# Expert gates of a PEER layer: two added 128-column products per token in place of one of 256 columns

## The chip, the cores and the metric

The kernel runs on one core of a Trainium2 chip. The core has TensorE (PE; its weight loads are the row PEld), VectorE (DVE), ScalarE (ACT), GpSimd (POOL), and SyncE (SP), which issues most transfers. The metric is the device time of one execution in microseconds. Before the change it was 1377.74 us in the median of 3 runs (1374.68 to 1379.49).

## The reference, cut to what matters

The program computes two transformer blocks for 256 tokens of width 1024. The last part of the second block is the PEER layer, a layer of 128 x 128 = 16384 experts:

```
s = einsum('thpd,hpkd->thpk', q, sub_keys)            # 8 heads, 2 halves, 128 keys
top_s, top_i = top_k(s, 16)
cand_s = top_s[:, :, 0, :, None] + top_s[:, :, 1, None, :]
cand_i = top_i[:, :, 0, :, None] * 128 + top_i[:, :, 1, None, :]
best_s, best_pos = top_k(cand_s, 16)                  # 8 x 16 = 128 picks per token
gate = softmax(best_s)
h = gelu(einsum('thkd,td->thk', u_table[idx], xb))
return einsum('thk,thkd->td', gate * h, v_table[idx])
```

Each pick is an expert (i, j) with a gate. All values are 32-bit floats.

## The kernel before, in words

For 224 of the 256 tokens (`TD`) the PEER layer is computed densely. `u_table` and `v_table` are read whole, as 128 items of 128 x 1024 each, one item for each value of j (for v: likewise). For each u item TensorE computes the pre-activations of 128 experts for 224 tokens; ScalarE applies gelu and writes them to the tile `HS`, which is 128 values of i on the partitions by 128 values of j by 224 tokens. Then `HS` must be multiplied by the gates, which are zero for all but the 128 picks of a token. The remaining 32 tokens are computed with gathered rows by GpSimd's indirect transfers and VectorE.

All products take 32-bit operands as a high part and a low part, since the fast product format keeps only some of the bits. An item of weights lands in `RAW` (a ring of 4 slots, transfers issued by SP at line 411), ScalarE makes its high part `WH` (line 1043 in this stage), GpSimd the low part `WL` (line 455), and TensorE does three products for each of the 8 chunks of 128 rows (line 1179): high x high, high x low, low x high, each with 224 columns. That is 24 products for an item.

The gates of a token are made as a product of one-hots (`gates_of`, line 1742). The contraction is over the token's 128 picks: `hot_i` has a 1 where the pick's i is, `hot_j` has the gate where the pick's j is. `hot_j` holds the gate's high part (VectorE, line 2546) and its low part (ScalarE, line 1019). One product per token has `hot_i` as the stationary operand and both parts of `hot_j`, side by side, as 256 moving columns, so that PSUM gets two halves of 128 columns that have still to be added.

The tokens are worked in groups of four, which I call a step: index c in the code, in two halves g of two tokens a. There are 224 / 4 = 56 steps. The order is written out by hand. In the last part of the u items (the one-hot stage) each item on TensorE has the four tokens of one step in its middle: 12 products of the item, 4 of one-hots, 12 of the item. TensorE's loop waits for `hot_low` (the low parts are there) and `gated` (VectorE is done with the step two before, whose PSUM banks are used again). ScalarE does in an item: the copy of the parked half of a step (`rest_high`, line 1010), the low parts (line 1019), the high part of an item (line 1043), and after each second item a gelu (line 995). VectorE does in a step the one-hots of the next (`one_hots`, lines 2543 and 2546), then `gate`: only 64 of the 128 values of j (`KEPT`) are multiplied at once, because `HS` holds items whose gelu is done; the other 64 are parked in a tile `stage` and in DRAM, and multiplied in the next stage.

In `gate` before the change VectorE sums the halves of the 64 kept j (line 2558, a reduction of 512 elements to 256 into PSUM bank 2), adds the low half of the 64 parked j to the copy of the high half that ScalarE has put into `stage` (line 2561), and multiplies `HS` by the sums (line 2563).

After this stage comes the v stage: 128 items, for each 8 pairs of products, one of 448 columns (line 1802) and one of 224 (line 1803).

Of the kernel before, what the change touches and what calls it, by code (L numbers as in the profile page):

```python
# [19 lines left out]
ALU = mybir.AluOpType  # L20
# [5 lines left out]
AX_X = mybir.AxisListType.X  # L26
# [24 lines left out]
PH, NK, TOPK = 8, 128, 16  # L51
# [9 lines left out]
KEPT = 64  # L61
# [88 lines left out]
def bass_blocks(nc, weights, x_in, p_in, vec_in, rows_in, gate_w_in, lora_in, mb_in, fb_in, out, rest_dram, x2_dram, u_rows):  # L150
    with ExitStack() as ctx:
# [158 lines left out]
        hot_i = at("hot_i", [P, 2, 2, P], F32R, C0 + 1024)  # L310

        hot_j = at("hot_j", [P, 2, 2, 2, NK], F32R, 0)
        stage = at("stage", [P, 2, NK - KEPT, 8], F32, 4096)
# [14 lines left out]
        PS = ctx.enter_context(nc.psum_tensor("PS", [P, 8, 512], F32))  # L328
# [6 lines left out]
        def sem(name):  # L335
            name = LATER[name][0] if name in LATER else name
            if name not in sems:
                sems[name] = ctx.enter_context(nc.semaphore(name))
            return sems[name]
# [44 lines left out]
            i = n - FIRST["keys"]  # L384
            return KK[:, 1, i, :] if 0 <= i < 2 else WL[:, n % RING, :]

        def made(c, part_):
            b = 4 + 2 * (c % 2)
            return PS[:, b:b + 2, :].rearrange("p b (a l j) -> p l j (b a)", a=2, l=2)[:, part_]

        def at_token(x, t):
            return x[:, t:t + 1] if isinstance(t, int) else x[:, bass.ds(t, 1)]
# [149 lines left out]
        def _(act):  # L542
# [107 lines left out]
            for e in range(2 * MH):  # L650
# [5 lines left out]
                for sb in range(NT):  # L656
                    last = A(WE[:, e % 2, sb, :], PS[:, 6 + h % 2, d * S:(d + 1) * S], ACT.Relu,
                             bias=AT[:, 2 * d + sb, h:h + 1])
# [346 lines left out]
            def rest_high(i, c, first=False):  # L1005

                act.wait_ge(sem("hot_used"), 8 * i + (2 * c + 2))
                if c % 2 == 0 and not first:
                    act.wait_ge(sem(f"parked{c // 2}"), 16 * i)
                nc.scalar.copy(stage[:, c // 2, :, 4 * (c % 2):4 * (c % 2) + 4],  # L1010
                               made(c, 0)[:, KEPT:NK]).then_inc(sem("rest_high"), 1)

            def hot_lows(i, c):

# [132 lines left out]
        def _(pe):  # L1147
# [584 lines left out]
            def gates_of(i, c, first=False):  # L1732

                if not first:

                    pe.wait_ge(sem("gated"), 4 * i + (c - 1))
                elif c >= 2:
                    pe.wait_ge(sem("gated"), c - 1)
                for g in range(2):
                    pe.wait_ge(sem("hot_low"), 8 * i + (2 * c + g + 1))  # L1740
                    for a in range(2):
                        last = mm(PS[:, 4 + 2 * (c % 2) + g, a * 2 * NK:(a + 1) * 2 * NK], hot_i[:, g, a, :],  # L1742
                                  hot_j[:, g, a, :, :], start=True, stop=True)
                    last.then_inc(sem("hot_used"), 1)

            def gates_behind(i, c):
# [114 lines left out]
        def _(dve):  # L1861
# [688 lines left out]
            def gate(i, c, first=False):  # L2550

                dve.wait_ge(sem("hot_used"), 8 * i + (2 * c + 2))
                hs = HS[:, 0:KEPT, tokens(16 * i + 4 * c, 4)]
                kept, parked = slice(0, KEPT), slice(KEPT, NK)
                dve.wait_ge(sem("rest_high"), 4 * i + (c + 1))
                b = 4 + 2 * (c % 2)
                sums = PS[:, 2, 2 * NK * (c % 2):2 * NK * (c % 2) + 4 * KEPT].rearrange("p (j a) -> p j a", a=4)
                V.tensor_reduce(sums, PS[:, b:b + 2, :].rearrange(
                    "p b (a l j) -> p j (b a) l", a=2, l=2)[:, kept], AX_X, ALU.add).then_inc(sem("sums_ready"), 1)
                rest = stage[:, c // 2, :, 4 * (c % 2):4 * (c % 2) + 4]  # L2560
                V.tensor_tensor(rest, rest, made(c, 1)[:, parked], ALU.add)
                dve.wait_ge(sem("sums_ready"), 4 * i + (c + 1))
                V.tensor_tensor(hs, hs, sums, ALU.mult).then_inc(sem("gated"), 1)

            def rest_block(r):

# [170 lines left out]
```

## Time and profile before

| | |
|---|---|
| median of 3 runs | 1377.74 us |
| the profiled execution's own time | 1376.38 us |
| its span in the trace | 1374.6 us |
| PE busy, of the span | 1337.0 us, 97% |
| DVE busy | 952.6 us, 69% |
| ACT busy | 848.9 us, 62% |
| POOL busy | 842.2 us, 61% |
| one-hot stage | 846.6 to 1027.4 us of the span |
| v stage | about 1029 to 1362 us |

The span is the stretch from the first to the last instruction in the trace; 1.8 us of the execution lie outside it. Matmuls are pipelined: the trace gives each a duration of 220 to 450 ns, but they start 60 to 240 ns apart, so that a mean duration is not what a product costs. What it costs is the distance from its start, or from the start of its weight load, to the next one's. An engine's busy time is the time in which at least one of its instructions is under way.

### The profile page before, as it was taken

The page shows a single profiled execution, that of the slowest core. Times are in us where ns is not written, and L with a number is a line of the kernel's source. Part 1 is how long each engine was busy: PE and PEld are TensorE (multiplying, and loading weights), DVE is VectorE, ACT ScalarE, POOL GpSimd, SP SyncE. Part 2 cuts the span into 40 slices and gives each one's busy share as a digit, 9 for nine tenths or more (in the row PEclk, how much of TensorE's full clock was granted, in tenths as well). Part 3 has the DMA queues.
Part 4 walks back from the last instruction along what each step waited for, and adds up shares of the span by engine and source line. Part 5 has one row for each costly group of instructions (what it writes and reads, how often), then busy time and mean ns, then how long its engine had stood idle before and what let it go on. Part 6 is the DMA issues. An engine that isn't in the chain of part 4 may idle for free.

```text
span 1374.6 us, 28810 instructions
## 1 busy us (share of the span) xinstructions
PE 1337.0 (97%) x9930; PEld 1215.8 (88%) x9930; DVE 952.6 (69%) x1998; ACT 848.9 (62%) x1463; POOL 842.2 (61%) x410
## 2 busy tenths in 40 slices
PE   7999999999999999989999989999999999999996
PEld 6878888888898777879999989999999999999996
DVE  3784884024674664453999465999997988888885
ACT  5475775445865656555777736888885554555553
POOL 7885888887675622867999848777772222233310
PEclk9999999999999999999999999999999999999998
DMA  6643555654443421655566577565657999898981
GB/s 205 206 135 126 172 197 196 196 189 156 167 158 116 143 78 46 214 185 167 186 200 196 187 291 257 200 201 198 204 199 286 345 365 369 310 331 315 328 290 61
DMA packets 83838, 287.68 MB, mean 209 GB/s; under 512 B 9656, under 2 KB 10040, under 8 KB 83512
## 3 DMA queue, kind: packets, MB, share of 16 engines
q1 hardware_dynamic: 64192, 231.76, 50.1%
q0 software_dynamic: 9216, 33.56, 6.3%
q10 hardware_dynamic: 10360, 21.43, 4.5%
q8 instruction: 43, 0.70, 0.2%
q14 instruction: 27, 0.22, 0.1%
HBM read 277.23 MB, written 9.44 MB: 209 GB/s over the span
## 4 chain that ended last, share of the span: by engine, by line
PE 64%; POOL 12%; issue 8%; DVE 7%; DMA 6%; ACT 1%; ACTq 0%; POOLq 0%; DVEq 0%; SPq 0%
PE PS L1179 37%; POOL WL L455 12%; PE PS L1802 10%; PE PS L1803 5%; DMA RAW<-weights 3%; PE PS L1742 2%; PE PS L1224 2%; DMA stage_odd<-gates_rest 2%; DVE WL L2636 2%; PE PS L1225 1%; PE PS L1561 1%; DVE gathered L2587 1%; DMA gathered<-u_rows,chosen 1%; PE PS L1519 0%; DVE XS L2417 0%
## 5 line engine op out<-in xcount | busy, mean ns | idle before, releaser
L455 POOL TENSOR_TENSOR WL<-RAW,WH 128x1024 fp32r<-128x1024 f32 x294 | 709.0, 2424 | 243.2 <-ACT WH L550 181.0
L1179 PE MATMUL PS<-XHL,WH 128*128 128x224 f32 (+1 forms) x2528 | 438.1, 278 | 8.6 <-DVE WL L2611 6.4
L1179 PEld LDWEIGHTS PS<-XHL,WH 128*128 128x128 f32 x2528 | 388.3, 193 | 12.4 <-DVE WL L2611 6.8
L1179 PE MATMUL PS<-XHL,WL 128*128 128x224 f32 (+1 forms) x1264 | 350.2, 277 | 0.0
L1802 PE MATMUL PS<-CHL,WH 128*128 128x448 f32 x1024 | 322.0, 375 | 1.4 <-DVE CHL L2575 1.4
L1803 PE MATMUL PS<-CHL,WL 128*128 128x224 f32 x1024 | 270.6, 264 | 0.0
L550 ACT CAST WH<-RAW 128x1024 fp32r<-128x1024 f32 x184 | 191.2, 1047 | 106.2 <-PE PS L1179 96.4
L1179 PEld LDWEIGHTS PS<-XHL,WL 128*128 128x128 f32 x1264 | 244.1, 193 | 0.0
L1084 ACT CAST WH<-RAW 128x1024 fp32r<-128x1024 f32 x128 | 134.8, 1053 | 150.3 <-PE PS L1803 80.3
L1802 PEld LDWEIGHTS PS<-CHL,WH 128*128 128x128 f32 x1024 | 192.1, 188 | 16.7 <-DVE CHL L2575 1.6
L1803 PEld LDWEIGHTS PS<-CHL,WL 128*128 128x128 f32 x1024 | 195.4, 191 | 0.0
L2636 DVE TENSOR_TENSOR WL<-RAW,WH 128x1024 fp32r<-128x1024 f32 x128 | 156.5, 1223 | 43.5 <-ACT WH L1084 42.7
L1043 ACT CAST WH<-RAW 128x1024 fp32r<-128x1024 f32 x124 | 129.0, 1043 | 64.3 <-PE PS L1179 51.7
L1224 PE MATMUL PS<-XHL,WH 128*128 128x512 f32 x384 | 138.4, 403 | 0.5 <-DVE XHL L2431 0.4
L511 POOL DMA_INDIRECT gathered<-weights,chosen x32 | 54.0, 1688 | 110.3 <-DVE sparse_y L2602 78.0
L1179 PE MATMUL PS<-WH,XHL 128*128 128x512 f32 x352 | 118.9, 402 | 0.6 <-POOL WL L455 0.4
L511 POOL DMA_INDIRECT gathered<-u_rows,chosen x32 | 51.1, 1597 | 109.5 <-DVE gathered L2587 100.7
L1225 PE MATMUL PS<-XHL,WL 128*128 128x256 f32 x384 | 108.1, 282 | 0.0
L1019 ACT ACTIVATE hot_j<-hot_j,GQ 128x128 fp32r<-128x128 f32 x224 | 78.0, 395 | 26.9 <-DVE hot_j L2546 25.4
L1224 PEld LDWEIGHTS PS<-XHL,WH 128*128 128x128 f32 x384 | 72.8, 190 | 18.3 <-issue 1.2
L1179 PEld LDWEIGHTS PS<-WH,XHL 128*128 128x128 f32 x352 | 66.5, 189 | 16.8 <-POOL WL L455 1.1
L2546 DVE TENSOR_SCALAR hot_j<-PS,JT,GH 128x128 fp32r<-128x128 f32 x224 | 80.6, 401 | 0.0
(433 smaller groups left out, 2120.5 us busy)
## 6 DMA issues: line engine op xcount, KB each, us to landing
RAW<-weights SPq DMA_DIRECT2D x438, 512.0 KB, 3.8
gates_rest<-stage ACTq DMA_DIRECT2D x28, 256.0 KB, 2.2
stage<-gates_rest ACTq DMA_DIRECT2D x7, 512.0 KB, 9.1
stage_odd<-gates_rest ACTq DMA_DIRECT2D x7, 512.0 KB, 8.2
H<-x SPq DMA_DIRECT2D x2, 512.0 KB, 4.5
LG<-rows ACTq DMA_DIRECT2D x2, 512.0 KB, 6.4
LB<-rows ACTq DMA_DIRECT2D x2, 512.0 KB, 9.2
x<-H ACTq DMA_DIRECT2D x1, 1024.0 KB, 5.7
```

The lines of the kernel that those rows point to most:

```text
L455: nc.gpsimd.tensor_tensor(WL[:, slot, :], RAW[:, slot, :], plain(WH[:, slot, :]), ALU.subtract).then_inc(w_lo, 1)
L511: nc.gpsimd.indirect_dma_start(out=gathered[:, n % ROWS, :], out_offset=None, in_=table, in_offset=bass.IndirectOffsetOnAxis(ap=chosen[:, ...
L550: nc.scalar.copy(high_of(n), RAW[:, slot, :]).then_inc(w_hi, 1)
L1043: nc.scalar.copy(WH[:, slot, :], RAW[:, slot, :]).then_inc(w_hi, 1)
L1084: nc.scalar.copy(WH[:, slot, :], RAW[:, slot, :]).then_inc(w_hi, 1)
L1179: last = mm(dst, a, b, start=start and k == 0, stop=stop and k == len(pairs) - 1)
L1224: mm(both, wh, XHL[:, :, k, :], start=(k == 0), stop=False)
L1225: last = mm(PS[:, bank, 0:S], wl, XH[:, k, :], start=False, stop=(k == KC - 1))
L1802: mm(PS[:, ch, 0:2 * TD], wh, CHL[c][:, :, :].rearrange("p a t -> p (a t)"), start=start, stop=False)
L1803: return mm(PS[:, ch, 0:TD], wl, CHL[c][:, 0, :], start=False, stop=stop)
L2546: last = V.tensor_scalar(hot_j[:, g, a, 0, :], iota_ps, at_token(JT, t + a), at_token(plain(GH), t + a), ALU.is_equal, ALU.mult)
L2636: V.tensor_tensor(WL[:, slot, :], RAW[:, slot, :], plain(WH[:, slot, :]), ALU.subtract).then_inc(w_lo, 1)
```

## The change

Each token gets two products of 128 columns in place of one of 256: both with the same stationary operand `hot_i`, the first with the high part of `hot_j`, the second with the low part, and the second adds to the same 128 columns of PSUM. The four tokens of a step then take one PSUM bank and not two, and what is in PSUM is the finished gate. So VectorE's reduction and its addition into `stage` go, and the multiplication reads PSUM's gates directly. ScalarE's copy into `stage` stays, of the same size, and now copies the finished gates. The helper `made` loses its argument for the half. The waits between the engines stay; only the one of VectorE for its own reduction (`sums_ready`) goes.

```diff
--- before.py
+++ after.py
@@ -384,9 +384,8 @@
             i = n - FIRST["keys"]
             return KK[:, 1, i, :] if 0 <= i < 2 else WL[:, n % RING, :]
 
-        def made(c, part_):
-            b = 4 + 2 * (c % 2)
-            return PS[:, b:b + 2, :].rearrange("p b (a l j) -> p l j (b a)", a=2, l=2)[:, part_]
+        def made(c):
+            return PS[:, 4 + c % 2, :].rearrange("p (a j) -> p j a", a=4)
 
         def at_token(x, t):
             return x[:, t:t + 1] if isinstance(t, int) else x[:, bass.ds(t, 1)]
@@ -1008,7 +1007,7 @@
                 if c % 2 == 0 and not first:
                     act.wait_ge(sem(f"parked{c // 2}"), 16 * i)
                 nc.scalar.copy(stage[:, c // 2, :, 4 * (c % 2):4 * (c % 2) + 4],
-                               made(c, 0)[:, KEPT:NK]).then_inc(sem("rest_high"), 1)
+                               made(c)[:, KEPT:NK]).then_inc(sem("rest_high"), 1)
 
             def hot_lows(i, c):
 
@@ -1739,8 +1738,9 @@
                 for g in range(2):
                     pe.wait_ge(sem("hot_low"), 8 * i + (2 * c + g + 1))
                     for a in range(2):
-                        last = mm(PS[:, 4 + 2 * (c % 2) + g, a * 2 * NK:(a + 1) * 2 * NK], hot_i[:, g, a, :],
-                                  hot_j[:, g, a, :, :], start=True, stop=True)
+                        made_at = PS[:, 4 + c % 2, (2 * g + a) * NK:(2 * g + a + 1) * NK]
+                        mm(made_at, hot_i[:, g, a, :], hot_j[:, g, a, 0, :], start=True, stop=False)
+                        last = mm(made_at, hot_i[:, g, a, :], hot_j[:, g, a, 1, :], start=False, stop=True)
                     last.then_inc(sem("hot_used"), 1)
 
             def gates_behind(i, c):
@@ -2551,16 +2551,8 @@
 
                 dve.wait_ge(sem("hot_used"), 8 * i + (2 * c + 2))
                 hs = HS[:, 0:KEPT, tokens(16 * i + 4 * c, 4)]
-                kept, parked = slice(0, KEPT), slice(KEPT, NK)
                 dve.wait_ge(sem("rest_high"), 4 * i + (c + 1))
-                b = 4 + 2 * (c % 2)
-                sums = PS[:, 2, 2 * NK * (c % 2):2 * NK * (c % 2) + 4 * KEPT].rearrange("p (j a) -> p j a", a=4)
-                V.tensor_reduce(sums, PS[:, b:b + 2, :].rearrange(
-                    "p b (a l j) -> p j (b a) l", a=2, l=2)[:, kept], AX_X, ALU.add).then_inc(sem("sums_ready"), 1)
-                rest = stage[:, c // 2, :, 4 * (c % 2):4 * (c % 2) + 4]
-                V.tensor_tensor(rest, rest, made(c, 1)[:, parked], ALU.add)
-                dve.wait_ge(sem("sums_ready"), 4 * i + (c + 1))
-                V.tensor_tensor(hs, hs, sums, ALU.mult).then_inc(sem("gated"), 1)
+                V.tensor_tensor(hs, hs, made(c)[:, 0:KEPT], ALU.mult).then_inc(sem("gated"), 1)
 
             def rest_block(r):
```

On TensorE, in the loop over the one-hot stage, this is the middle of one item and its step of one-hots. `XHL` is the activations' high and low part, `WH` and `WL` the item's; a row without a count is one instruction. Before:

```order
L1179 MATMUL PS<-XHL,WH 128x224 x2
L1179 MATMUL PS<-XHL,WL 128x224
L1736 ISA
L1740 ISA
L1742 MATMUL PS<-hot_j,hot_i 128x256 x2
L1740 REGISTER_ALU
L1742 MATMUL PS<-hot_j,hot_i 128x256 x2
L1179 MATMUL PS<-XHL,WH 128x224 x2
L1179 MATMUL PS<-XHL,WL 128x224
```

In the changed program the same place reads (line numbers are one less, as the file is shorter):

```order
L1178 MATMUL PS<-XHL,WL 128x224
L1735 ISA
L1739 ISA
L1742 MATMUL PS<-hot_j,hot_i 128x128
L1743 MATMUL PS<-hot_j,hot_i 128x128
L1742 MATMUL PS<-hot_j,hot_i 128x128
L1743 MATMUL PS<-hot_j,hot_i 128x128
L1739 REGISTER_ALU
L1742 MATMUL PS<-hot_j,hot_i 128x128
L1743 MATMUL PS<-hot_j,hot_i 128x128
L1742 MATMUL PS<-hot_j,hot_i 128x128
L1743 MATMUL PS<-hot_j,hot_i 128x128
```

Four products have become eight; the waits (ISA, REGISTER_ALU) stand where they stood.

On VectorE, in the loop over the same stage, this is the end of one set of one-hots and `gate` of the step before. Before:

```order
L2546 TENSOR_SCALAR hot_j<-PS,JT,GH 128x128
L2555 ISA
L2558 TENSOR_REDUCE PS<-PS 128x256
L2561 TENSOR_TENSOR stage<-stage,PS 128x64x4
L2563 REGISTER_ALU
L2563 TENSOR_TENSOR HS<-HS,PS 128x64x4
L2540 REGISTER_ALU
```

In the changed program:

```order
L2546 TENSOR_SCALAR hot_j<-PS,JT,GH 128x128
L2554 ISA
L2555 REGISTER_ALU
L2555 TENSOR_TENSOR HS<-HS,PS 128x64x4
L2540 REGISTER_ALU
```

The reduction and the addition are gone, and the multiplication comes right behind the one-hots.

## Rows read from the trace of the kernel before

**Rows 1.** Page, part 1: busy time, share, instructions.

```profile
PE 1337.0 (97%) x9930; PEld 1215.8 (88%) x9930; DVE 952.6 (69%) x1998; ACT 848.9 (62%) x1463; POOL 842.2 (61%) x410
```

**Rows 2.** Stretches: window, length, busy time per engine, granted clock, DMA share, GB/s.

```profile
846.60:1027.38 180.78, 180.60 (x1548) 176.88 (x1548) 178.28 (x495) 155.31 (x360) 131.87 (x55) 1.00 0.59 198
...
1120.00:1160.00 40.00, 40.00 (x257) 38.18 (x257) 32.77 (x47) 19.28 (x29) 9.46 (x7) 1.00 0.99 375
```

**Rows 3.** Waits, 846 to 1030 us: total us, times, longest.

```profile
PEld PS L1742 <- ACT hot_j L1019: 2.8, 13, 0.3
...
DVE hot_i L2543 <- PE PS L1742: 1.1, 3, 0.7
```

**Rows 4.** Groups of instructions, 846 to 1030 us: busy us, mean ns | idle before.

```profile
L1179 PE MATMUL PS<-XHL,WH 128*128 128x224 f32 x902 | 153.7, 274 | 0.0
L1179 PEld LDWEIGHTS PS<-XHL,WH 128*128 128x128 f32 x902 | 137.2, 192 | 0.0
...
L1742 PE MATMUL PS<-hot_j,hot_i 128*128 128x256 f32 x224 | 42.5, 300 | 0.2
L2558 DVE TENSOR_REDUCE PS<-PS 128x256 f32<-128x512 f32 x56 | 38.5, 687 | 1.3 <-ACT stage L1010 1.3
L1742 PEld LDWEIGHTS PS<-hot_j,hot_i 128*128 128x128 f32 x224 | 33.0, 190 | 3.9 <-ACT hot_j L1019 2.8
L2561 DVE TENSOR_TENSOR stage<-stage,PS 128x256 f32<-128x256 f32 x56 | 22.9, 408 | 0.0
```

**Rows 5.** Chain that ended last, 867 to 883 us: start, us, what.

```profile
869.59 0.53 PE PS L1742 x4
870.12 2.67 PE PS L1179 x24
872.79 0.24 PE PS L1742 x2
873.03 0.03 issue
873.06 0.51 PE PS L1742 x2
...
876.24 0.53 PE PS L1742 x4
...
879.44 0.62 PE PS L1742 x4
```

**Rows 6.** Weight loads in order of time, end of the v stage: start, us.

```profile
1355.79 0.14 PEld L1835 LDWEIGHTS PS<-unit,dense_y 128*128 128x128 f32 x1
1355.90 0.30 PEld L1836 LDWEIGHTS PS<-unit,dense_y 128*128 128x128 f32 x2
1356.12 0.19 PEld L1802 LDWEIGHTS PS<-CHL,WH 128*128 128x128 f32 x1
1356.23 0.19 PEld L1803 LDWEIGHTS PS<-CHL,WL 128*128 128x128 f32 x1
```

**Rows 7.** The same view at 606 us, products of 256 and 128 columns alternating.

```profile
606.04 0.19 PEld L1718 LDWEIGHTS PS<-KK,QH 128*128 128x128 f32 x1
606.16 0.19 PEld L1719 LDWEIGHTS PS<-KK,QL 128*128 128x128 f32 x1
...
606.51 0.19 PEld L1224 LDWEIGHTS PS<-XHL,WH 128*128 128x128 f32 x1
```

**Rows 8.** The same view in the v stage, pairs of 448 and 224 columns.

```profile
1100.07 0.19 PEld L1802 LDWEIGHTS PS<-CHL,WH 128*128 128x128 f32 x1
...
1102.89 0.19 PEld L1802 LDWEIGHTS PS<-CHL,WH 128*128 128x128 f32 x1
```

**Rows 9.** VectorE in order of time, 878 to 880 us.

```profile
878.59 0.69 DVE L2558 TENSOR_REDUCE PS<-PS 128x256 f32<-128x512 f32 x1
879.19 0.41 DVE L2561 TENSOR_TENSOR stage<-stage,PS 128x256 f32<-128x256 f32 x1
879.52 0.41 DVE L2563 TENSOR_TENSOR HS<-HS,PS 128x256 f32 x1
879.85 0.41 DVE L2543 TENSOR_TENSOR hot_i<-PS,IT 128x256 fp32r<-128x256 f32 x1
```

## The prediction

> **What bounds the kernel now.** I first read the page's busy times: PE is busy 97% of the span, DVE 69% [rows 1]. A share over the whole span doesn't say what bounds the stage of the change, so I next read that stage alone, as a window. From the first one-hot product at 846.6 us to the end of the last at 1027.38 us PE is busy 180.60 of 180.78 us, and DVE 178.28 [rows 2]. The reader is to see two things in that row: PE has no idle time left, and DVE nearly none, so either could set the pace. DMA is at 0.59 of its share there, so no transfer does.
>
> The view of waits tells the two apart only in part. PE's weight loads wait 2.8 us in total for the low parts of `hot_j`, in 13 places, one in four of the 56 steps; DVE waits 1.1 us for PE [rows 3]. The chain of waits shows the pattern. It runs on PE: 24 products of an item take 2.67 us, then come the four of one-hots, and four successive steps of these take 0.53, 0.24 + 0.03 + 0.51 = 0.78, 0.53 and 0.62 us [rows 5]. That is 2.46 us for four steps. With 4 x 2.67 = 10.68 it makes 13.14 us for four steps, and 14 times that is 184 us, which agrees with the window's 180.78 (its first item is cut off). So PE sets the pace, and in one step of four it waits a quarter of a microsecond for one-hots that DVE and ACT bring late.
>
> DVE's own pace, from start to start: the reduction 879.19 - 878.59 = 0.60 us, the addition 0.33, the multiplication 0.33 [rows 9]. That the step's other work fills the rest follows from DVE being busy 178.28 us, 3.2 us for each of 56 steps; PE's is 180.78 / 56 = 3.2 too. The two are matched to within some hundredths of a microsecond, which is why PE's waits are so small.
>
> **What a product costs.** All rests on this. A matmul's mean duration (300 ns for one-hots [rows 4]) isn't its cost, as the next starts long before it ends. I take distances from start to start.
> - An item's products, 224 columns: 2.67 / 24 = 111 ns [rows 5].
> - 448 and 224 columns in turn: nine pairs from 1100.07 to 1102.89 us, 313 ns a pair, so some 202 ns for 448 columns if the 224 take 111 [rows 8]. Beyond 224 columns the cost grows by (202 - 111) / 224 = 0.41 ns a column.
> - 128 columns: at the end of the v stage one transposition and two ordinary products of 128 columns stand in a row. Their three weight loads and that of the next product start from 1355.79 to 1356.12 us, 0.33 / 3 = 110 ns each [rows 6]. In the stage of scores, 256 and 128 columns in turn, four loads take 606.51 - 606.04 = 0.47 us, 117 ns each [rows 7].
>
> So between 128 and 256 columns the cost is nearly flat, 110 to 120 ns: 128 columns are not cheaper than 224. What is common to these products is the weight load of 128 columns; there is one for every product, even where two in a row have the same stationary operand, as an item's first two have (902 loads for 902 products with `WH` [rows 4]; the two are high x high and high x low).
>
> I take 110 ns for a new product, the value of the row that is nearest in shape (128 columns, same stationary size, on a busy PE at full granted clock). The bounds are 71 ns below (the column price of [rows 8] carried on down from 224: 111 - 96 x 0.41) and 130 ns above (the one-hots' own 0.53 / 4 in an undisturbed step [rows 5], wait included).
>
> The Trainium skill's page "TensorE: Matmul & The Clock Gate", section "LDWEIGHTS (loading the stationary operand)", gives the load as columns by 1.2 GHz, an estimate of 107 ns for 128 columns; by it eight products cost 0.86 us. The same page's section "Back-to-back issue gap" speaks against that: it has 81 ns for each load and product of 128 columns in a sustained stream, and by it the eight would cost 0.65 us; the row of three 128-column products, at 110 ns, agrees with the first and not with the second. What hangs on the second is the rival of cheap products below.
>
> **The change part by part.**
> 1. TensorE: 224 products of 256 columns become 448 of 128. In a step, the undisturbed 0.53 us for four is 4 x 117 ns (the price in [rows 7]) and 0.06 us of issue and semaphores between the halves. Eight at 110 ns with the same 0.06 make 0.94 us. The step with 0.62 us has some 0.09 us more, put down to nothing that waits; I keep that once in four steps. Four steps: 4 x 0.94 + 0.09 = 3.85 us, against 2.46. That is 1.39 us more for four steps, if the wait of [rows 3] goes, and x 14 = 19.5 us.
> 2. VectorE: the reduction and the addition go, 0.60 + 0.33 = 0.93 us of a step [rows 9]; in busy time that is part of 38.5 + 22.9 us [rows 4]. DVE then needs 3.2 - 0.93 = 2.27 us for a step, against 2.67 + 0.94 = 3.61 us on PE. It is no longer near the bound, so the saving itself is worth nothing but the wait that goes: 0.78 - 0.53 = 0.25 us in one step of four, 3.5 us in 14, which the sum of point 1 has already taken in. Worth of this edit at the least 0, at the most 3.5 us.
> 3. Could the one-hots be late in another way? `hot_i` and `hot_j` have a buffer per half. PE now frees the first half 0.47 us after it begins a step and the second after 0.94. DVE's two halves of one-hots take (3.2 - 0.60 - 0.33 - 0.33) / 2 = 0.97 us each, so they are made by 0.47 + 1.94 = 2.4 us, and ACT's two low parts of the second half are there some 1 us later, 3.4. PE asks for them at 3.61 + 0.47 = 4.1. That leaves 0.7 us, room for ACT's gelu (0.53 us) ahead of them. It's enough, so I forecast no wait; if the quarter microsecond stays after all, 3.5 us are to be added.
> 4. The multiplication reads PSUM with the tokens 128 elements apart, and not in a row. The addition that goes read PSUM in just that way, and takes as long, 0.33 us to the next [rows 9]. Cost 0; if it doubled, DVE still had a microsecond of room.
> 5. ScalarE's copy has the same size; cost 0. The PSUM write of the second product adds onto the first's columns right behind it; an item's 24 products all do that at 111 ns, so 0.
> 6. After the stage: the v stage is PE's too (40.00 of 40.00 us [rows 2]), and starts after the last u item, so a longer stage moves it as a whole. DMA is at 0.99 of its share there, but the ring of four items can't carry transfers ahead from a stage that has DMA to spare. Nothing is given back, at most 1 to 2 us of odd waits.
>
> Sum against the profiled execution's own 1376.38 us: + 19.5 - 1 (half of the odd waits) = 1394.9 us. The median of the runs is 1.4 us above that execution, so in the runs' terms it is 1396.2. I say 1395.5.
>
> **The rivals.**
> - *Cheap products.* The weight load hides behind the product before, and cost follows columns down to 71 ns. Then a step's eight take 0.57 + 0.06, four steps 4 x 0.63 + 0.09 = 2.61 us, + 0.15 x 14 = 2 us: 1378.5 us, no measurable change. For it: the column price of [rows 8] holds above 224. Against it: [rows 6]. By the skill's 81 ns it would be an estimate of + 6.6 us, from the page "TensorE: Matmul & The Clock Gate". Chance 4%, and 3% for a value between the two prices, up to + 12 us.
> - *Faster.* The second product of a token has the stationary operand that is loaded already. If that load cost nothing, a token's pair would cost what its 256 columns cost now, four steps 4 x 0.53 + 0.09 = 2.21 us against 2.46, since DVE's relief takes PE's wait away: - 3.5 us, 1372.9 us. It decides from where the second product costs less than about 15 ns beyond the first. Against it: 902 loads for 902 products, and 111 ns each in the items, where two in three have the same case. Chance 3%.
> - *Dearer products.* The new ones cost as much as the present 256-column ones in place, 130 ns, with the waits kept: four steps 4 x 8 x 0.13 + 0.09 + 0.25 = 4.50 us, + 2.04 x 14 = 28.6 us, 1405 us. For it: the one-hots are the only products here that are spaced 130 ns. Against it: that spacing has the issue gap in it. Chance 8%.
> - *Relief that counts.* The change does what its words say and DVE, not PE, sets the pace. Then 56 x 0.93 = 52 us would go. PE's 180.60 of 180.78 us rule it out; it gets nothing beyond the 3% above.
>
> **How the numbers follow.** The forecast (+ 15 to + 23 us) has 82%: 1391 to 1400. The range for 8 in 10 takes a part of the dearer case and a little below: 1388 to 1401. A difference under 0.3%, 4 us, can't be told from no change. Slower by more than that: 82 + 8 + most of the 3 between = 92%. Within it: 5%. Faster: 3%.
>
> **What would show it.** In the changed profile: 448 one-hot loads and products; in the chain pieces of 0.9 to 1.0 us for eight products between pieces of 2.67 us; the one-hot stage near 199 us with PE still busy throughout, DVE at some 130 us (2.27 x 56); the wait for `hot_j` gone; the v stage as long as before. Wrong would be: weight loads of one-hots 55 to 80 ns apart (cheap products), fewer loads than products (faster), a new wait of PE on ACT, or a v stage that is shorter by what the stage before lost.

## The result, and the profile after

The changed kernel takes 1393.8 us in the median of 4 runs (1391.31 to 1394.9), against 1378.47 us for the kernel before (4 runs). The ratio is 1.0121, with a 95% interval of 1.01 to 1.0142: it is slower by 15.3 us. The forecast was 1395.5 us, 1.7 above the measured median, and inside its range of 1388 to 1401. The sum behind it, + 18.5 us, was 3.2 us too large.

The profiled execution took 1391.31 us, with a span of 1389.6 us. This is the busy line of its page.

```profile
PE 1351.9 (97%) x10154; PEld 1235.2 (89%) x10154; DVE 904.9 (65%) x1886; ACT 851.7 (61%) x1463; POOL 843.1 (61%) x410
```

Against [rows 1], TensorE has 224 instructions more and 14.9 us more busy time, VectorE 112 instructions and 47.7 us less. A twentieth of VectorE's work is gone, and the kernel is slower by about the time that was added to TensorE's.

The stage itself, as a window from the first one-hot product to the last (window, length, busy time of PE, weight loads, DVE, ACT and POOL, granted clock, DMA share, GB/s), answers to [rows 2]:

```profile
846.10:1043.90 197.80, 197.80 (x1772) 197.66 (x1771) 129.63 (x385) 158.98 (x361) 133.41 (x57) 1.00 0.55 184
```

It is 17 us longer. DVE has fallen from 178.28 to 129.63 us, and PE has no gap at all; even its weight loads now fill the window (197.66 of 197.80, against 176.88 of 180.78). The waits of the stage (total us, times, longest), which answer to [rows 3], have turned round. VectorE now waits for TensorE in all but one of its steps, and the wait of TensorE for `hot_j` is no longer in the view:

```profile
DVE hot_i L2543 <- PE PS L1743: 66.8, 55, 1.4
```

The groups of the stage (busy us, mean ns | idle before) that answer to [rows 4]:

```profile
L1743 PE MATMUL PS<-hot_j,hot_i 128*128 128x128 f32 x224 | 53.2, 276 | 0.0
...
L1743 PEld LDWEIGHTS PS<-hot_j,hot_i 128*128 128x128 f32 x224 | 43.0, 192 | 0.0
L1742 PEld LDWEIGHTS PS<-hot_j,hot_i 128*128 128x128 f32 x224 | 43.0, 192 | 0.1
```

448 products and 448 loads: the second product of a token loads the same stationary operand again. What each costs is best seen in the weight loads in order of time (start, us), a whole step of one-hots between two parts of an item:

```profile
878.25 0.19 PEld L1178 LDWEIGHTS PS<-XHL,WL 128*128 128x128 f32 x1
878.37 0.19 PEld L1742 LDWEIGHTS PS<-hot_j,hot_i 128*128 128x128 f32 x1
878.48 0.19 PEld L1743 LDWEIGHTS PS<-hot_j,hot_i 128*128 128x128 f32 x1
...
879.15 0.19 PEld L1743 LDWEIGHTS PS<-hot_j,hot_i 128*128 128x128 f32 x1
879.26 0.30 PEld L1178 LDWEIGHTS PS<-XHL,WH 128*128 128x128 f32 x2
```

From 878.37 to 879.26 are eight loads in 0.89 us, 0.11 us each. There is no gap between the two halves, where a wait stands in the program: the wait costs nothing when what it waits for is there. The chain of waits agrees with it; its pieces of 24 products (start, us) now come at a steady distance:

```profile
872.34 2.72 PE PS L1178 x24
...
875.91 2.72 PE PS L1178 x24
...
879.49 2.72 PE PS L1178 x24
```

3.57 us a step, that is 32 products at 111.7 ns. Before, four steps took 13.14 us, 3.28 each [rows 5].

What TensorE waited for before is plainer in the weight loads than in the view of waits, which lists only the longer gaps. Two steps of the kernel before: the low parts of the second half on ScalarE, and the first load of that half on TensorE (start, us).

```profile
882.00 0.69 ACT L1019 ACTIVATE hot_j<-hot_j,GQ 128x128 fp32r<-128x128 f32 x2 [0.27 <-DVE hot_j L2546]
882.75 0.30 PEld L1742 LDWEIGHTS PS<-hot_j,hot_i 128*128 128x128 f32 x2
```

```profile
885.43 0.70 ACT L1019 ACTIVATE hot_j<-hot_j,GQ 128x128 fp32r<-128x128 f32 x2 [0.28 <-DVE hot_j L2546]
886.18 0.30 PEld L1742 LDWEIGHTS PS<-hot_j,hot_i 128*128 128x128 f32 x2 [0.22 <-ACT hot_j L1019]
```

ScalarE is done at 882.69 and at 886.13, and TensorE goes on 0.05 us later both times. It is so in 54 of the 56 steps of the kernel before, not in one of four. The second load of a first half and the first of the second are there 0.17, 0.27, 0.17 and 0.42 us apart in turn, against 0.12 where nothing is late (e7 below): 0.5 us of waiting in four steps. In the changed kernel it is so in one step of 56, and the low parts lie ready 0.34 us early.

**The balance.** I take for each run the first weight load of the one-hots, the last of them, and the first and last of the v stage (L1802). Before: 846.5, 1027.0, 1036.5 and 1360.5 us. After: 846.0, 1043.5, 1053.0 and 1375.5. So the one-hot stage up to the v stage went from 190.0 to 207.0 us, + 17.0. The part ahead of it differs by - 0.5, the v stage by 322.5 - 324.0 = - 1.5, the end by 0. The sum is + 15.0 us, the difference of the spans. The v stage was 323.1 to 326.7 us in the runs below, whatever they changed, and 323.1, 324.5 and 326.1 in three that share the changed kernel's v stage and pace (e2, e3, e6), so I take its - 1.5 for scatter and not for an effect of the change. The one-hot stage up to the v stage scatters far less: 206.97 to 207.02 us in the changed kernel and those three.

### The profile page after: what moved, and what is told of

The parts are those of the page before. It is cut to its first block, busy times and chain, and to the rows that moved or that the text cites. A ratio compares the mean times of both kernels' runs of the same rounds, so it can differ in the third digit from the quotient of the medians.

```text
span 1389.6 us, 29146 instructions
## 1 busy us (share of the span) xinstructions
PE 1351.9 (97%) x10154; PEld 1235.2 (89%) x10154; DVE 904.9 (65%) x1886; ACT 851.7 (61%) x1463; POOL 843.1 (61%) x410
## 4 chain that ended last, share of the span: by engine, by line
PE 60%; DVE 2%; DMA 1%; ACTq 0%; issue 0%; ACT 0%; POOL 0%; DVEq 0%
PE PS L1178 27%; PE PS L1802 15%; PE PS L1803 7%; PE PS L1223 2%; PE PS L1743 2%; PE PS L1742 2%; PE PS L1224 1%; DMA gathered<-u_rows,chosen 1%; DVE XS L2417 0%; PE PS L1518 0%; PE PS L1717 0%; PE PS L1527 0%; PE PS L1539 0%; DVE H L2423 0%; DMA x_late<-x 0%
## 5 line engine op out<-in xcount | busy, mean ns | idle before, releaser
L1802 PE MATMUL PS<-CHL,WH 128*128 128x448 f32 x1024 | 321.6, 374 | 0.3 <-DVE CHL L2567 0.3
L1802 PEld LDWEIGHTS PS<-CHL,WH 128*128 128x128 f32 x1024 | 192.0, 188 | 15.1 <-DVE WL L2628 0.6
L1223 PE MATMUL PS<-XHL,WH 128*128 128x512 f32 x384 | 138.0, 402 | 0.7 <-DVE XHL L2431 0.6
L2543 DVE TENSOR_TENSOR hot_i<-PS,IT 128x256 fp32r<-128x256 f32 x112 | 46.9, 419 | 78.4 <-PE PS L1743 66.8
```

The source lines that it names most:

```text
L1223: mm(both, wh, XHL[:, :, k, :], start=(k == 0), stop=False)
L1802: mm(PS[:, ch, 0:2 * TD], wh, CHL[c][:, :, :].rearrange("p a t -> p (a t)"), start=start, stop=False)
```

## The experiments

Each run is compared with the kernel before on the same chip, which took 1375 to 1377 us there. "Step" is the mean distance between two steps of one-hots, from the first to the last weight load, less what lies within a step, over 55. The column "to v" is the one-hot stage up to the v stage in the profiled execution, as in the balance above.

| run | step, us | DVE busy in 150 us | to v, us | median, us | ratio to before (95%) |
|---|---|---|---|---|---|
| before | 3.28 | 148.5 | 189.96 | | 1 |
| changed kernel | 3.58 | 98.9 | 207.02 | 1393.8 | 1.0121 (1.01 to 1.0142) |
| e1 before, no sums | 3.25 | 109.3 | 188.63 | 1373.5 | 0.9981 (0.9972 to 0.9991) |
| e2 changed, sums kept | 3.58 | 138.0 | 206.97 | 1391.67 | 1.0119 (1.0094 to 1.0144) |
| e3 changed, 64 moving | 3.58 | 99.1 | 206.98 | 1392.5 | 1.0129 (1.0112 to 1.0146) |
| e4 changed, 64 stationary | 3.25 | 109.4 | 188.70 | 1374.11 | 0.9989 (0.9976 to 1.0002) |
| e5 changed, one product | 3.21 | 110.4 | 186.53 | 1372.63 | 0.998 (0.9966 to 0.9993) |
| e6 changed, interleaved | 3.58 | 99.0 | 206.98 | 1391.34 | 1.012 (1.0097 to 1.0143) |
| e7 before, products twice | 3.63 | 136.2 | 209.94 | 1393.59 | 1.0145 (1.0125 to 1.0164) |
| e8 before, ScalarE copies | 3.27 | 149.8 | 189.84 | 1375.36 | 1.0008 (0.9995 to 1.002) |
| e9 before, halves apart | 3.24 | 148.4 | 187.90 | 1374.25 | 0.9985 (0.9971 to 1.0) |
| e10 no sums, halves apart | 3.16 | 112.3 | 183.34 | 1369.9 | 0.9948 (0.9931 to 0.9965) |
| e11 e8, halves apart | 3.25 | 150.0 | 188.74 | 1376.12 | 0.999 (0.9974 to 1.0005) |
| e12 e11, sums in PSUM | 3.16 | 143.7 | 183.34 | 1368.49 | 0.9958 (0.9943 to 0.9973) |

The diffs are shortened: rearrangements of slices, semaphore increments and the lines that only follow from an edit are left out, and where both products of a token are changed alike, one is shown.

### What a one-hot product costs: e3, e4, e6, e7

**e3.** 64 moving columns in each product.

```diff
-mm(made_at, hot_i[:, g, a, :], hot_j[:, g, a, 0, :], start=True, stop=False)
+mm(made_at, hot_i[:, g, a, :], hot_j[:, g, a, 0, 0:64], start=True, stop=False)
```

> The changed kernel with 64 moving columns in each of the 448 one-hot products and not 128 (the gates of the 64 parked j are left out). Load theory: a product costs its weight load of 128 columns, 111.7 ns, so no change against the changed kernel (within 1 us), and the loads are still 0.11 us apart. Column theory: 0.41 ns a column, 26 ns a product, -11.8 us.

Half the columns change nothing: the step is 3.58 us, and the loads (start, us) of this run are as far apart as with 128:

```profile
902.24 0.19 PEld L1742 LDWEIGHTS PS<-hot_j,hot_i 128*128 128x128 f32 x1
902.35 0.19 PEld L1743 LDWEIGHTS PS<-hot_j,hot_i 128*128 128x128 f32 x1
...
903.13 0.30 PEld L1178 LDWEIGHTS PS<-XHL,WH 128*128 128x128 f32 x2
```

Eight in 0.89 us. The column theory is out in this range: from 64 to 224 moving columns a product costs the same.

**e4.** 64 stationary columns.

```diff
-made_at = PS[:, 4 + c % 2, (2 * g + a) * NK:(2 * g + a + 1) * NK]
-mm(made_at, hot_i[:, g, a, :], hot_j[:, g, a, 0, :], start=True, stop=False)
+made_at = PS[0:64, 4 + c % 2, (2 * g + a) * NK:(2 * g + a + 1) * NK]
+mm(made_at, hot_i[:, g, a, 0:64], hot_j[:, g, a, 0, :], start=True, stop=False)
```

> The changed kernel with 64 stationary columns (half of hot_i; the gates of the other 64 i are left out) and 128 moving ones in each one-hot product. Load theory: the load takes half as long, so a product falls to what 128 moving columns or the shorter load ask for, 60 to 75 ns: 448 x 37 to 52 ns = 16 to 23 us less than the changed kernel, 1371 to 1377. Column theory, and a theory by which a fixed cost per instruction sets the 111 ns: no change.

The same view of this run:

```profile
901.13 0.14 PEld L1743 LDWEIGHTS PS<-hot_j,hot_i 128*64 128x64 f32 x1
901.19 0.13 PEld L1742 LDWEIGHTS PS<-hot_j,hot_i 128*64 128x64 f32 x1
901.25 0.13 PEld L1743 LDWEIGHTS PS<-hot_j,hot_i 128*64 128x64 f32 x1
```

Half the stationary columns, and the products come 0.06 us apart. So it is the weight load that costs, not an instruction as such. By the ratios (0.9989 against 1.0121) the run is some 18 us shorter than the changed kernel. It ought to be more: 448 x 52 ns is 23 us. Part of the difference is that the second of a step's eight loads still comes 0.11 us after the first (901.13, after one at 901.02), and only the seven distances behind it are 0.06. So PE's own work is 24 x 111.7 + 107 + 7 x 60 ns = 3.21 us, and the step fell only to 3.25. These last 0.04 us are a wait, to which the round trip below comes back.

**e6.** No two neighbours with the same stationary operand (`l` is the part, high or low; the two tokens are in two banks).

```diff
-for a in range(2):
-    mm(made_at, hot_i[:, g, a, :], hot_j[:, g, a, 0, :], start=True, stop=False)
-    last = mm(made_at, hot_i[:, g, a, :], hot_j[:, g, a, 1, :], start=False, stop=True)
+for l in range(2):
+    for a in range(2):
+        last = mm(made_at, hot_i[:, g, a, :], hot_j[:, g, a, l, :], start=l == 0, stop=l == 1)
```

> The changed kernel with the four products of a half in the order high of token 0, high of token 1, low of token 0, low of token 1 (the two tokens in two PSUM banks, since an open sum must not share a bank with a new one). Nothing is left out. No two neighbours have the same stationary operand. Load theory: no change against the changed kernel (within 1 us). If a repeated stationary operand gets a discount in the changed kernel: slower, by up to 224 x 40 ns = 9 us.

No change, and the loads are again 111 to 112 ns apart: a repeated stationary operand has no discount. The rival of a free second load is out.

**e7.** 448 products of 256 columns.

```diff
-last = mm(PS[:, 4 + 2 * (c % 2) + g, a * 2 * NK:(a + 1) * 2 * NK], hot_i[:, g, a, :],
-          hot_j[:, g, a, :, :], start=True, stop=True)
+for _ in range(2):
+    last = mm(PS[:, 4 + 2 * (c % 2) + g, a * 2 * NK:(a + 1) * 2 * NK], hot_i[:, g, a, :],
+              hot_j[:, g, a, :, :], start=True, stop=True)
```

> The kernel before with each 256-column one-hot product made twice (the second overwrites the first with the same values): 448 products as in the changed kernel, but of 256 columns, and VectorE's sums stay. Load theory: a 256-column product costs 117 ns, set by its columns; a step is 24 x 111.3 + 8 x 117 = 3.61 us and the waits for hot_j are gone, 56 x (3.61 - 3.274) = 19 us more than before, 2 to 4 us more than the changed kernel. Column theory (what costs is columns): 448 x 53 ns = 24 us more than the changed kernel.

The chain of waits of this run (start, us, what):

```profile
868.98 0.95 PE PS L1743 x8
869.93 2.67 PE PS L1179 x24
872.60 0.95 PE PS L1743 x8
```

Eight of 256 columns take 0.95 us, 119 ns each, with no gap between the halves. The step of 3.63 us is what the load theory said (3.61), and twice the columns cost 56 x 0.05 = 3 us more than the changed kernel's stage (209.94 against 207.02 up to the v stage), not the 24 us of the column theory. In the whole time that can't be told apart: the ratios, 1.0145 and 1.0121, have intervals that overlap.

### What VectorE's work is worth: e1, e2, e5

**e2.** VectorE's two instructions put back into the changed kernel.

```diff
+V.tensor_reduce(sums, PS[:, 4 + c % 2, :].rearrange("p (n l) -> p n l", l=2), AX_X, ALU.add)
+V.tensor_tensor(rest, rest, made(c)[:, KEPT:NK], ALU.max)
 V.tensor_tensor(hs, hs, made(c)[:, 0:KEPT], ALU.mult).then_inc(sem("gated"), 1)
```

> The changed kernel with a reduction of 512 elements and a two-operand instruction on the parked gates (a maximum with themselves) put back on VectorE, in their old places; results unchanged. VectorE needs some 3.2 us a step again, PE 3.575. Load theory: PE sets the pace, no change against the changed kernel (within 1 us). If VectorE's relief were a part of what the changed kernel's stage costs, it would be slower: by up to 3.5 to 7.5 us, with a wait of PE for hot_j back in the trace.

DVE is busy 138.0 us of 150, against 98.9, and the step is the same 3.58 us. In the changed kernel what VectorE was relieved of is worth nothing.

**e1.** The relief alone, in the kernel before.

```diff
-V.tensor_reduce(sums, PS[:, b:b + 2, :].rearrange(...)[:, kept], AX_X, ALU.add)
-V.tensor_tensor(rest, rest, made(c, 1)[:, parked], ALU.add)
-V.tensor_tensor(hs, hs, sums, ALU.mult).then_inc(sem("gated"), 1)
+V.tensor_tensor(hs, hs, made(c, 0)[:, kept], ALU.mult).then_inc(sem("gated"), 1)
```

> The kernel before with VectorE's reduction (L2558) and its addition into stage (L2561) left out, so the low halves of the gates are not used; TensorE's products are those of before. It takes the change's relief of VectorE alone. Lateness theory: all that a step's one-hots cost beyond 4 x 117 ns (0.604 - 0.47 = 0.13 us a step) is PE waiting for VectorE and ScalarE, so the step falls from 3.274 to 3.14 us, the wait for hot_j goes, and the run is 7.5 us shorter than before (1371). Gap theory: 0.06 us a step and 0.09 in one of four are a fixed cost of the semaphores on PE; only the 0.25 us in one step of four goes: -3.5 us. If VectorE's relief is worth nothing: 0.

A quarter of VectorE's work in the stage is gone, and the run gains 2.6 us (ratio 0.9981), of which its profiled execution shows 1.3 in the stage (188.63 against 189.96). That is near what the gap theory said, but the trace fits neither theory whole. The chain (start, us, what) alternates:

```profile
900.30 0.49 PE PS L1742 x4
...
903.46 0.66 PE PS L1742 x4
...
906.78 0.49 PE PS L1742 x4
```

4 x 119 = 0.48 us is the products' own time, so in one step there is no gap, and in the next one of 0.17 us. A fixed cost of semaphores would be in every step. And VectorE isn't late because it has too much work: it waits 48.2 us for PE in this stage (`hot_i`, 54 times).

**e5.** One product of 128 columns per token, in the changed kernel.

```diff
-mm(made_at, hot_i[:, g, a, :], hot_j[:, g, a, 0, :], start=True, stop=False)
-last = mm(made_at, hot_i[:, g, a, :], hot_j[:, g, a, 1, :], start=False, stop=True)
+last = mm(made_at, hot_i[:, g, a, :], hot_j[:, g, a, 0, :], start=True, stop=True)
```

> The changed kernel with the high part's product alone, 128 columns once per token (the low parts of the gates are left out): 224 products fewer. Load theory: each costs 111.7 ns, so 25 us less than the changed kernel, and 24 x 111.7 + 4 x 111.7 = 3.13 us a step, some 8 us less than the kernel before. If a second product with the same stationary operand were cheaper than a first (60 to 70 ns): only 14 to 16 us less than the changed kernel.

The expectation missed: I had a step of 3.13 us and 25 us less than the changed kernel. The step is 3.21, and by the ratios (0.998 against 1.0121) the gain is some 19 us. TensorE's work is at 28 x 111.7 ns = 3.13 us. So, as in e1 and e4, something other than TensorE's and VectorE's work holds the step at 3.21 to 3.25 us.

### The round trip of a half: e9, e10

VectorE and ScalarE of e5 in order of time (start, us), from one step to the next, show what it is.

```profile
905.68 0.42 DVE L2542 TENSOR_TENSOR hot_i<-PS,IT 128x256 fp32r<-128x256 f32 x1 [0.90 <-PE PS L1742]
906.02 0.72 DVE L2545 TENSOR_SCALAR hot_j<-PS,JT,GH 128x128 fp32r<-128x128 f32 x2
906.66 0.41 DVE L2542 TENSOR_TENSOR hot_i<-PS,IT 128x256 fp32r<-128x256 f32 x1
906.99 0.72 DVE L2545 TENSOR_SCALAR hot_j<-PS,JT,GH 128x128 fp32r<-128x128 f32 x2
```

```profile
907.84 0.69 ACT L1018 ACTIVATE hot_j<-hot_j,GQ 128x128 fp32r<-128x128 f32 x2 [0.27 <-DVE hot_j L2545]
```

```profile
905.08 0.54 PEld L1742 LDWEIGHTS PS<-hot_j,hot_i 128*128 128x128 f32 x4
908.22 0.67 PEld L1742 LDWEIGHTS PS<-hot_j,hot_i 128*128 128x128 f32 x4
```

The load of the second half in the last row, by itself:

```profile
908.59 0.30 PEld L1742 LDWEIGHTS PS<-hot_j,hot_i 128*128 128x128 f32 x2
```

TensorE begins its step at 905.08. VectorE waits until the first half is free and starts at 905.68; it makes both halves, one behind the other, until 907.7. ScalarE makes the low parts of the second half from 907.84 to 908.53, and TensorE, which began the next step at 908.22, has to wait for them (four loads take 0.67 us, not 0.54). That is a closed round trip: TensorE frees the first half, VectorE fills it and then the second, ScalarE fills the second's low part, TensorE uses it. From the load of a first half (905.08) to that of the next step's second half (908.59) it takes 3.51 us, and in all of e5's steady steps it takes that (in e1 3.57), however little work any one engine has. TensorE's own work between the two loads is 30 products, 3.35 us, so it has to wait.

The wait doesn't come in full in every step. A first half is loaded 26 products, 2.90 us, after the second half before it, so a long wait at one second half delays the next first half, but not the next second half, which hangs on the first half before. Two steps so take 3.51 + 2.90 = 6.41 us, 3.2 each, with a longer and a shorter gap in turn, as e1's chain has them. The second half's load comes 0.05 us after ScalarE's low parts in 53 of the 56 steps of e5, and in as many of e1 and of e4, so this is the wait that is left in all three.

If so, more room for the second half must help, with no work taken from anyone. e9 and e10 move its two products 6 products later in the item. The waits in the program stay the same three.

```diff
-if k == KC // 2 and c in gates:
-    gates_behind(i, c)
+if k == KC // 2 and c in gates:
+    gates_behind(i, c, [0])
+if k == 6 and c in gates:
+    gates_behind(i, c, [1])
```

**e9**, in the kernel before:

> The kernel before with the second half's two one-hot products moved 6 products later in the item (behind chunk 5, not behind chunk 3). Round-trip theory: the bubbles on TensorE come from the round trip of a half, PE frees it, VectorE makes both halves, ScalarE the low parts, PE uses it, 3.24 us; moving the second half gives it 0.45 us of room, but VectorE still works 3.2 us in a step, so the step falls from 3.27 to 3.20 at best: 0 to -4 us against before. Gap theory (a fixed cost of semaphores on PE, one more place to wait): 0 to +3 us.

**e10**, the same in e1:

> The same move in the kernel of e1 (the kernel before without VectorE's sums; low halves of the gates not used). Nothing but the round trip and PE's own work is left. Round-trip theory: the step falls from the 3.24 us of e1 to PE's own 24 x 111.3 + 4 x 117 = 3.14, -5.6 us against e1, and the bubbles of 0.16 us in every second step go. Gap theory: the step stays at 3.24 or grows, as there is one more place with a wait.

The chain of e10 (start, us, what):

```profile
900.70 0.25 PE PS L1743 x2
900.94 2.00 PE PS L1179 x18
902.94 0.24 PE PS L1743 x2
903.19 0.66 PE PS L1179 x6
903.85 0.25 PE PS L1743 x2
```

Every pair takes 0.24 to 0.25 us, two products and nothing more, and the step is 3.15 us here, 3.16 in the mean. e10's interval (0.9931 to 0.9965) lies clear of e1's (0.9972 to 0.9991): by the ratios it is 4.5 us shorter, and up to the v stage 5.3 us (183.34 against 188.63). That settles it: the gaps in e1 were the round trip. The gap theory with its fixed cost is out, since e10 has the same waits in the program and no gap. (Both expectations speak of one more place to wait; the code has none, the wait for the second half's low parts moves with its products.)

e9 gains little (0.9985, to 1.0; 2.1 us up to the v stage), as VectorE is still busy 148.4 of 150 us. In the kernel before three limits lie within 0.1 us of each other: TensorE's own work 3.16 us (e10), VectorE's pace 3.24 (e9) and the round trip 3.25 (e1). With the last two in one kernel the step is 3.28. All of this waiting, 0.12 us a step and 6.6 us up to the v stage, lies inside a TensorE that the profile shows busy 180.60 of 180.78 us: a matmul's time in the profile covers most gaps of this size, so a full busy share doesn't show that an engine sets the pace alone.

### A version that beats both: e8, e11, e12

TensorE has the cheapest form before the change; what can be saved is VectorE's reduction. VectorE takes 0.60 us for it [rows 9], and 0.33 for an addition of the same number of results. So that the addition takes one half from SBUF, as the one into `stage` does, ScalarE copies it there.

```diff
+nc.scalar.copy(kept_high(c), made(c, 0)[:, 0:KEPT].rearrange(...))
 nc.scalar.copy(stage[:, c // 2, :, 4 * (c % 2):4 * (c % 2) + 4], made(c, 0)[:, KEPT:NK])
...
-V.tensor_reduce(sums, PS[:, b:b + 2, :].rearrange(...)[:, kept], AX_X, ALU.add)
+V.tensor_tensor(kept_high(c), kept_high(c), made(c, 1)[:, kept], ALU.add)
...
-V.tensor_tensor(hs, hs, sums, ALU.mult)
+V.tensor_tensor(hs, hs, kept_high(c), ALU.mult)
```

> A version meant to beat both: TensorE's products as before; ScalarE also copies the high halves of the kept gates to SBUF, into unused columns of XHL (256 elements, 0.33 us a step more), so that VectorE adds the low halves with an addition of 256 elements (0.33 us) in place of the reduction (0.60). VectorE 3.2 - 0.27 = 2.93 us a step, ScalarE 2.8 + 0.33 = 3.1, PE 3.14 plus waits. If VectorE was what made PE wait: -3.5 to -7 us against before. If ScalarE's order (its gelu ahead of the low parts) makes PE wait: no change, or up to 5 us slower, as ScalarE is now the fullest after PE.

**e11** is e8 with the halves apart:

> The same move in the kernel of e8 (ScalarE copies the kept high halves, VectorE adds instead of reducing; nothing left out), a version meant to beat both kernels. Round-trip theory: VectorE needs 2.93 us a step, ScalarE 3.1, PE 3.14; the step falls to 3.15 to 3.20 us: -4 to -7 us against before (1369 to 1372). If ScalarE, now nearly full and in fixed order, sets the pace: no change against e8, within 2 us of before.

Neither moved the time by anything that can be measured, for a reason that neither expectation had. VectorE is full, 149.8 and 150.0 us of 150, though it should have 2.93 us of work in a step. Its multiplication of `HS`, now with both operands in SBUF, grew, to a median of 0.97 us in e11 and 0.79 in e8. First the row of that line in e11 (min/median/max ns, first and last start), then VectorE and GpSimd in order of time:

```profile
L2571 DVE TENSOR_TENSOR HS<-HS,kept_all x56: 406/966/1340, 847.9 to 1026.9; 128x256 f32 x52, 128x256 f32<-128x256 f32 x4
```

```profile
903.85 0.43 DVE L2571 TENSOR_TENSOR HS<-HS,kept_all 128x256 f32 x1
...
906.80 1.08 DVE L2571 TENSOR_TENSOR HS<-HS,kept_all 128x256 f32 x1
```

```profile
901.58 2.42 POOL L459 TENSOR_TENSOR WL<-RAW,WH 128x1024 fp32r<-128x1024 f32 x1 [0.54 <-ACT WH L1048]
905.19 2.42 POOL L459 TENSOR_TENSOR WL<-RAW,WH 128x1024 fp32r<-128x1024 f32 x1 [1.19 <-ACT WH L1048]
```

At 906.80 GpSimd is in the middle of its subtraction, which ends at 907.61, and the multiplication ends at 907.88, just behind it. At 903.85 GpSimd is about to end (904.00), and the multiplication takes 0.43 us. Every multiplication of the stage that took over 0.43 us, 29 of 56 in e11 and 53 of 56 in e8, ended 0.28 to 0.29 us after GpSimd's subtraction, whenever it had begun. In the kernel before, where the sums are in PSUM, it takes 0.41 [rows 9], with a subtraction under way too.

The Trainium skill has this on its page "SBUF — State Buffer", section "SBUF: two separate sides": a VectorE instruction with two SBUF inputs and a GpSimd instruction that reads SBUF need the same pair of ports, and the one that starts first holds it for its whole length. The trace agrees for a multiplication that starts second; the other order isn't shown here.

**e12** is e11 with the sums written to PSUM:

```diff
-V.tensor_tensor(kept_high(c), kept_high(c), made(c, 1)[:, kept], ALU.add)
+V.tensor_tensor(kept_sums, kept_high(c), made(c, 1)[:, kept], ALU.add)       # PSUM bank 2
-V.tensor_tensor(hs, hs, kept_high(c), ALU.mult)
+V.tensor_tensor(hs, hs, kept_sums, ALU.mult)
```

> The kernel of e11 with VectorE's addition of the kept halves written to PSUM (bank 2, as the sums of the kernel before), not back to SBUF; nothing left out. In e8 and e11 the multiplication of HS by the sums in SBUF took 0.4 us in some steps and 1.0 us in others (median 0.97 in e11, 0.79 in e8), and ended when GpSimd's subtraction did. Port theory: with a PSUM operand it takes 0.41 us always, VectorE falls to 2.93 us a step, and with the halves apart the step nears TensorE's 3.14: 3.15 to 3.20, -4 to -7 us against before. If ScalarE's 3.1 us a step in fixed order is what counts, the step stays at 3.2 us or above and the run within 3 us of before, as e11.

Its multiplication's row, and its stretch from 860 to 1010 us in the columns of [rows 2]:

```profile
L2573 DVE TENSOR_TENSOR HS<-HS,PS x56: 410/414/422, 847.9 to 1021.3; 128x256 f32 x52, 128x256 f32<-128x256 f32 x4
```

```profile
860.00:1010.00 150.00, 150.00 (x1334) 150.00 (x1334) 143.69 (x429) 143.93 (x357) 114.31 (x48) 1.00 0.62 209
```

The multiplication takes 0.41 us again, and the step is 3.16 us, TensorE's own work. That rules out ScalarE's fixed order as what held e11 up: ScalarE does the same work here, 143.9 us of 150. The run takes 1368.49 us in the median of 12 against 1375.41, ratio 0.9958 (0.9943 to 0.9973), where e11 had 0.9974 to 1.0005, and up to the v stage it is 183.34 us against e11's 188.74. It leaves nothing out and is faster than both kernels, by 0.4% than the one before.

## Why the prediction was right

**What bounds the stage.** Held for the changed kernel, and only in part for the one before. TensorE sets the pace after the change, with no wait. Before it, TensorE had 3.16 us of work in a step of 3.28, and its second half waited for ScalarE's low parts in 54 of 56 steps. I had read that wait from the view of waits as one step in four and from TensorE's full busy time as next to nothing. I added that VectorE's pace lay within hundredths of TensorE's. e1 and e10 show a third limit just there, which I hadn't put into words as a limit: the round trip. I had worked its times out (point 3 of the change) only to ask whether it would make the changed kernel wait. The answer, no, held, with less room than I gave it: in a steady step of the changed kernel the low parts of the second half are there 3.68 us after the step before began (881.94 to 885.62), not 3.4, and TensorE asks for them at 4.02, so that 0.34 us are left of my 0.7.

**What a product costs.** Held, and it carried the forecast. I took 110 ns from the three 128-column products of [rows 6]; it is 111.7. That the moving columns don't matter was read from [rows 6] and [rows 7], and e3 (64 columns, no change) and e4 (half the stationary columns, 60 ns) show that the weight load is what is paid. The estimate from the Trainium skill's page "TensorE: Matmul & The Clock Gate", section "LDWEIGHTS (loading the stationary operand)", 107 ns for a load, came near. The 81 ns of the same page's section "Back-to-back issue gap" are not what the trace shows: the 448 products are 111.7 ns apart.

**The size.** Forecast + 19.5 us in the stage, measured + 17.0. What was mis-sized is in point 1: the 0.06 us "of issue and semaphores between the halves" in each step and the 0.09 us in one step of four, both of which I took for fixed costs of TensorE and carried over. In the changed kernel eight products take 0.89 us and nothing besides. The 0.06 and 0.09 were the same wait for the second half's low parts as the quarter microsecond, made by the round trip and by VectorE's own pace together. It vanishes as soon as TensorE's own step is longer, which e7 shows for the 256-column product too (0.95 us for eight). Of the 0.5 us of it in four steps I let only 0.25 go. Carried over, they had put 56 x 0.06 + 14 x 0.09 = 4.6 us too much into the stage; 448 x 1.7 ns, 0.8 us, were too little. That makes 15.7; of the 1.3 us to 17.0, some 0.5 are the items' own products, 111.7 ns and not 111.3 (1344 of them), and some 0.6 come from this, that four steps before took 13.10 us in the mean and not 13.14.

That the stated time came nearer than the sum, 1.7 us against 3.2, is luck. In the runs' terms the sum gave 1396.2 us, and I wrote 1395.5 for no reason that the working has; and the kernel before was 0.7 us slower in the median of four runs than in the three I had.

**The relief of VectorE.** Held: worth nothing in the changed kernel (e2), and in the kernel before 2.6 us by itself (e1), within my 0 to 3.5. With the round trip eased too it is worth more: e10 against e9 is 5.1 us by the ratios, 4.6 up to the v stage.

**After the stage.** I had allowed 1 us of odd waits to go; the v stage of the profiled execution was 1.5 us shorter, which is scatter between runs and no support for that term.

**The rivals.** Cheap products: out by e3 and e4. Faster by a free second load: out by e6 and by the 448 loads. Dearer products, 130 ns each: out, 111.7. VectorE sets the pace: out by e2, and by e1 for all but 2.6 us of the 52. The reason I gave, TensorE busy 180.60 of 180.78 us, would not have been enough: 6.6 us of waiting lay inside it.

## What to carry to other kernels

Where products are paced by their weight load, a narrower product is no cheaper: here 64 to 224 moving columns cost the same 0.112 us, so one product of 256 columns split into two of 128 costs nearly twice. Use the width that the load pays for anyway, and add the halves up on an engine that has time. When three engines pass one buffer round, work out its round trip as a limit beside each engine's work, and read waits from the starts of single instructions, not from busy time: moving one half's products by 6 places took away gaps that removing a quarter of VectorE's work had left.

## What the runs showed of the hardware

- With a load of 128 columns at full granted clock, products of 64, 128 and 224 moving columns start 111.7 ns apart (e3 and the changed kernel), those of 256 columns 119 (e7), in this stage. With a load of 64 columns and 128 moving ones it is 60 ns (e4).
- The same stationary operand twice in a row is loaded twice, at the full price (e6).
- VectorE's instruction with two SBUF inputs, 256 elements, took 0.41 us or up to 1.34 us, depending on whether GpSimd's subtraction of two SBUF tiles was under way; when held up it ended 0.28 us after it. With one input in PSUM it took 0.41 to 0.42 us in all 56 steps (e11, e12).
- A wait for a semaphore between two products cost TensorE nothing when what it waited for was there (eight products in 0.89 us across it, changed kernel), and 0.05 us passed from ScalarE's end to TensorE's load when it was not (before, e1, e4, e5).
